# Value products ahead of the turning: one move in the order of TensorE's work in a sparse-attention loop

## The chip, the cores and the metric

The kernel runs on one core of one Trainium2 chip. The metric is the device time of one launch in microseconds (us). Before the change three runs gave 3794.74, 3799.57 and 3803.0 us, with a median of 3799.57. One execution was profiled; it took 3797.03 us, and its span, from the first recorded instruction to the last, is 3795.2 us. All numbers of the trace are from that execution.

## The reference

Two transformer blocks run on 512 tokens of width 1024. The first has a state-space branch and dilated attention; the second has two layers, each a feed-forward part, a token mixer and another feed-forward part. The token mixer computes a gated delta rule and a sparse attention from one projection of the input. The change lies in one part of the sparse attention: for a block of 128 queries, softmax attention over the keys of that block and those before it, in two forms (selected keys and a window), added to a third, compressed form:

```python
ss = jnp.einsum("bqgrd,bqgld->bgrql", qb, k_sel) * scale
p_sel = masked_softmax(ss, (tok <= t[:, None])[:, :, None])
o_sel = jnp.einsum("bgrql,bqgld->bqgrd", p_sel.astype(v_sel.dtype), v_sel)
sw = jnp.einsum("bqgrd,bkgd->bgrqk", qb, k_win) * scale
p_win = masked_softmax(sw, win_mask)
o_win = jnp.einsum("bgrqk,bkgd->bqgrd", p_win.astype(v_win.dtype), v_win)
o = gb[..., 0:1] * o_cmp + gb[..., 1:2] * o_sel + gb[..., 2:3] * o_win
```

With 512 tokens and 16 selected blocks of 64, every causal key is selected, and the window of 512 reaches all of them too; so both forms read the keys 0 to 128(qb+1) under one causal mask.

## The kernel before

Each engine has a program of its own, written out by hand in the order in which it runs; semaphores connect them, and an engine waits at the first instruction whose semaphore is not there. The function `pe_mix` is TensorE's program of the token mixer, `act_mix` ScalarE's and `dve_mix` VectorE's. They run once in each of the two layers.

The sparse attention is cut into 32 steps (`nsa_blocks`, `work`): four query blocks `qb`, four pairs of heads `j`, two forms `i`. Query block `qb` has n = qb + 1 key blocks of 128, so steps 0 to 7 have one key block, 8 to 15 two, 16 to 23 three and 24 to 31 four. Two heads run side by side (G = 0, 1). The work of step v goes through four engines' stages:

- `scores(v)`, L1868, TensorE: q times k into the PSUM banks `g[2]` and `g[3]`. It waits for `row_max` of step v-1, which tells that the banks have been read.
- `maxima(v)`, L2533, VectorE: masks the scores into `n_p` and takes the negative row maxima into `n_stat` (a custom instruction and a read of its accumulator, once for each G).
- `probs(v)`, L2253, ScalarE: exponentials in place in `n_p`, with their sums.
- `turned(v)`, L1879, TensorE: transposes the probabilities into `p[0]` and `p[1]`. It waits for the exponentials and for the copies of step v-1 (`n_tr0`, `n_tr1`).
- the copies of the transposes into `n_pt`: of G = 0 on ScalarE (L2261), of G = 1 on VectorE (L2568).
- `weighted(v)`, L1889, TensorE: probabilities times values into `p[2]` or `p[3]`. It waits for VectorE's adding of step v-2.
- `added(v)`, L2574 to L2585, VectorE: three small operations on the sums, then two that add the result to `n_y`.

The stages of neighbouring steps overlap. In loop step s TensorE issues `scores(s)`, `turned(s-1)`, `feed(("core", s))` and `weighted(s-2)`. VectorE issues `maxima(s)`, the copy of s-1, `convolved(("core", s))` and `added(s-2)`; after each query block it also squares and sums `n_y`. ScalarE issues the copy of s-1, `probs(s)` and `taps(("core", s))`.

`feed` puts pieces of another work between these: the projection of twelve channels of the delta rule, L364 to L366, three products of 512 columns for each of eight input blocks of a channel. A loop step takes one input block of it, from step 16 on two (`mix_points`). A channel is completed in steps 7, 15, 19, 23, 27 and 31. Then ScalarE scales it (`taps`, L2189) and, after every second channel, in steps 15, 23 and 31, splits the next weights (L358), whose low part POOL then makes (L350); VectorE convolves it with three long operations (`convolved`, L2441), which wait for ScalarE's scaling.

Of the kernel before, what the change touches and what calls it, by code (L numbers as in the profile page):

```python
# [1781 lines left out]
def nsa_blocks():  # L1782

    return [(qb, j, i) for qb in range(NB) for j in range(4) for i in range(2)]
# [34 lines left out]
def pe_mix(K, pe, pos):  # L1819
# [3 lines left out]
    work = nsa_blocks()  # L1823
# [6 lines left out]
    def feed(name):  # L1830
        for j in points.get(name, ()):
            h, k = j // KD, j % KD
            s, n = h // 2 % 2, h % 2
            if k == 0:
                if n == 0:
                    pe.wait_ge(K.sem("w_lo"), pos.next("w_lo"))
                pe.wait_ge(K.sem(f"g_free{n}"), pos.next(f"g_free{n}"))
            w = slice(k * 256 + n * P, k * 256 + n * P + P)
            last = three_pass(K, K.g[n][:], K.w_hi[:, s, w], K.w_lo[:, s, w], K.h_hi[:, k], K.h_lo[:, k], k == 0, k == KD - 1)
            if k == KD - 1:  # L1840
                last.then_inc(K.sem("part"), 1)
# [19 lines left out]
    def scores(v):  # L1861
        qb, j, i = work[v]
        w = (qb + 1) * P
        if v:
            pe.wait_ge(K.sem("row_max"), pos.next("row_max", 2))
        for G in range(2):
            r = slice(64 * G, 64 * G + 64)
            t.matmul(K.g[2 + G][:, 0:w], K.n_q[r, j, qb * P:qb * P + P], K.n_k[r, 2 + i, 0:w],  # L1868
                     start=True, stop=True).then_inc(K.sem("scores"), 1)

    def turned(v):
        n = work[v][0] + 1
        for G in range(2):
            pe.wait_ge(K.sem("n_pe"), pos.next("n_pe"))
            if v:
                pe.wait_ge(K.sem(f"n_tr{G}"), pos.next(f"n_tr{G}"))
            for k in range(n):
                o = G * n * P + k * P
                last = t.transpose(K.p[G][:, k * P:k * P + P], K.n_p[:, v % 2, o:o + P], ident)  # L1879
            last.then_inc(K.sem(f"n_pt{G}"), 1)  # L1880

    def weighted(v):
        qb, j, i = work[v]
        if v >= 2:
            pe.wait_ge(K.sem("n_acc"), pos.next("n_acc"))
        for G in range(2):
            pe.wait_ge(K.sem(f"n_tr{G}"), pos.value(f"n_tr{G}") + (1 if v == len(work) - 1 else 0))
            for k in range(qb + 1):
                last = t.matmul(K.p[2 + v % 2][:, 64 * G:64 * G + 64], K.n_pt[:, v % 2, 4 * G + k],  # L1889
                                K.m_v[:, k, P * i + 64 * G:P * i + 64 * G + 64], start=k == 0, stop=k == qb)  # L1890
        last.then_inc(K.sem("n_o"), 1)
# [125 lines left out]
    for step in range(len(work) + 2):  # L2017
        if 1 <= step < len(work):
            scores(step)
        if 1 <= step <= len(work):  # L2020
            turned(step - 1)
        feed(("core", step))
        if step >= 2:
            weighted(step - 2)
    pos.skip("row_max", 2)
    pos.skip("n_tr0")
    pos.skip("n_tr1")
# [699 lines left out]
def ffn_parts(conv, i, ada, norm, following):  # L2727
# [13 lines left out]
    ffn_c=ffn_parts(False, 2, lambda layer: None, lambda layer: Norm(layer, 2),  # L2741
                    lambda layer: Norm(layer + 1, 0) if layer + 1 < LAYERS else FINAL),
    mix=(pe_mix, act_mix, dve_mix), final=(pe_final, act_final, dve_final))
PE_PARTS, ACT_PARTS, DVE_PARTS = ({k: v[i] for k, v in PARTS.items()} for i in range(3))

# [184 lines left out]
```

## Time and profile before

| | |
|---|---|
| median of three runs | 3799.57 us |
| profiled execution | 3797.03 us, span 3795.2 us |
| TensorE busy | 3651.1 us, 96% of the span |
| VectorE, ScalarE, POOL busy | 1820.7, 1408.6, 1402.6 us |
| sparse-attention loop, layer 1 | about 1894 to 2021 us |
| sparse-attention loop, layer 2 | about 3092 to 3220 us |

A line of the trace names the engine (PE TensorE, PEld its weight loads, DVE VectorE, ACT ScalarE), the line of the kernel, the operation, the tile written and those read, and the shapes. A start is in us from the span's start; in brackets stands how long the engine had been idle, and what ended it. A busy time of neighbouring matmuls overlaps by some hundredths, so lengths are best read from start to start.

### The profile page before, as it was taken

The numbers are of one execution on the slowest core, as the hardware profiler recorded it, in microseconds if no ns is written. First come the engines' busy times: TensorE is split into PE (matmuls) and PEld (weight loads), VectorE is DVE, ScalarE is ACT, GpSimd is POOL, SyncE is SP. The second block draws the span as 40 slices with busy tenths as digits, with TensorE's granted clock in tenths as the row PEclk, the third lists the DMA queues.
The fourth block names the chain that finished last, engine by engine and source line by source line (L and its number), as shares of the span: only waits on it lengthen the run. The fifth ranks groups of instructions, "written<-read, shape, count | busy, mean of one in ns | idle before, by whom it ended". The sixth has DMA issues, their size and how long they took to land.

```text
span 3795.2 us, 48784 instructions
## 1 busy us (share of the span) xinstructions
PE 3651.1 (96%) x18948; PEld 3027.2 (80%) x18948; DVE 1820.7 (48%) x3285; ACT 1408.6 (37%) x2037; POOL 1402.6 (37%) x1092
## 2 busy tenths in 40 slices
PE   6999999999999999999998999999999989899998
PEld 5887878777788888887777978888888877888887
DVE  6887426665788664455375441123112457443111
ACT  5665424444322232223245432223222334533222
POOL 2333443223444444444211044455445411114444
PEclk9999999999999999999999999999999989999999
DMA  3211222111455655566100022223222401002222
GB/s 118 78 67 67 92 92 75 56 67 56 144 181 186 212 198 182 182 213 186 48 34 34 12 95 94 90 99 112 100 84 105 133 34 34 23 34 100 92 91 106
DMA packets 67647, 380.25 MB, mean 100 GB/s; under 512 B 7920, under 2 KB 8432, under 8 KB 39408
## 3 DMA queue, kind: packets, MB, share of 16 engines
q1 hardware_dynamic: 44192, 286.14, 21.2%
q10 hardware_dynamic: 23248, 91.19, 7.3%
q8 instruction: 149, 2.44, 0.3%
q14 instruction: 58, 0.48, 0.0%
HBM read 375.20 MB, written 2.10 MB: 99 GB/s over the span
## 4 chain that ended last, share of the span: by engine, by line
issue 62%; POOL 29%; PE 9%; POOLq 0%; DVE 0%; ACT 0%; DVEq 0%
POOL w_lo L350 29%; PE g L364 3%; PE g L365 3%; PE g L366 3%; POOLq L344 0%; DVE x L1696 0%; POOLq L347 0%; PE p L518 0%; PE p L510 0%; DVE x L1454 0%; DVE n_sq L497 0%; DVEq L155 0%; ACT n_sq L482 0%; POOLq L350 0%; ACT n_rc L525 0%
## 5 line engine op out<-in xcount | busy, mean ns | idle before, releaser
L350 POOL TENSOR_TENSOR w_lo<-w_raw,w_hi 128x512 fp32r<-128x512 f32 (+1 forms) x1088 | 1402.4, 1320 | 2386.3 <-ACT w_hi L358 2386.3
L364 PE MATMUL g<-h_hi,w_lo 128*128 128x512 f32 x2816 | 1135.6, 403 | 23.4 <-POOL w_lo L350 21.1
L365 PE MATMUL g<-h_lo,w_hi 128*128 128x512 f32 x2816 | 1106.7, 393 | 0.0
L366 PE MATMUL g<-h_hi,w_hi 128*128 128x512 f32 x2816 | 1106.3, 393 | 0.0
L358 ACT ACTIVATE w_hi<-w_raw 128x2048 fp32r<-128x2048 f32 (+1 forms) x292 | 515.8, 1766 | 968.6 <-PE g L366 931.8
L364 PEld LDWEIGHTS g<-h_hi,w_lo 128*128 128x128 f32 x2816 | 535.9, 190 | 144.3 <-POOL w_lo L350 24.4
L366 PEld LDWEIGHTS g<-h_hi,w_hi 128*128 128x128 f32 x2816 | 534.8, 190 | 115.6
L365 PEld LDWEIGHTS g<-h_lo,w_hi 128*128 128x128 f32 x2816 | 536.0, 190 | 109.9 <-issue 4.1
L364 PE MATMUL g<-act_hi,w_lo 128*128 128x512 f32 x880 | 346.0, 393 | 0.0
L366 PE MATMUL g<-act_hi,w_hi 128*128 128x512 f32 x880 | 342.9, 390 | 0.0
L365 PE MATMUL g<-act_lo,w_hi 128*128 128x512 f32 x880 | 342.5, 389 | 0.0
L1642 DVE TENSOR_TENSOR p<-f_acc,g 128x512 f32<-128x512 f32 x84 | 58.4, 696 | 566.5 <-PE g L366 565.3
L1490 DVE SCALAR_TENSOR_TENSOR p<-ada_w,csilu,p 128x256 f32<-128x256 f32 x432 | 211.7, 490 | 54.8 <-DMA ada_w<-in_ada 31.8
L366 PEld LDWEIGHTS g<-act_hi,w_hi 128*128 128x128 f32 x880 | 165.2, 188 | 35.4
L365 PEld LDWEIGHTS g<-act_lo,w_hi 128*128 128x128 f32 x880 | 165.4, 188 | 33.4
L364 PEld LDWEIGHTS g<-act_hi,w_lo 128*128 128x128 f32 x880 | 165.3, 188 | 33.3
L1454 DVE SCALAR_TENSOR_TENSOR x<-g,mods,x 128x512 f32<-128x512 f32 x48 | 36.0, 749 | 276.7 <-PE g L366 276.3
L1572 ACT ACTIVATE f_acc<-g 128x512 f32<-128x512 f32 x84 | 50.2, 598 | 258.8 <-PE g L366 250.2
L1621 DVE TENSOR_TENSOR act_lo<-p,act_hi 128x512 fp32r<-128x512 f32 x110 | 76.1, 692 | 119.2 <-ACT act_hi L1553 108.1
L497 DVE TENSOR_TENSOR n_sq<-n_sq 128x512 f32<-128x512 f32 x63 | 66.7, 1058 | 70.6 <-ACT n_sq L482 70.5
L482 ACT ACTIVATE n_sq<-x 128x512 f32<-128x512 f32 x72 | 44.9, 624 | 144.9 <-DVEq L1617 69.2
L1889 PEld LDWEIGHTS p<-m_v,n_pt 128*128 128x128 f32 x640 | 82.4, 194 | 8.5 <-DVE n_y L2585 3.3
(463 smaller groups left out, 4805.8 us busy)
## 6 DMA issues: line engine op xcount, KB each, us to landing
w_raw<-in_stream SPq DMA_DIRECT2D x212, 1024.0 KB, 4.8
ada_w<-in_ada ACTq DMA_DIRECT2D x144, 512.0 KB, 4.0
w_raw<-in_stream SPq DMA_DIRECT2D x80, 704.0 KB, 4.0
n_w<-in_w ACTq DMA_DIRECT2D x8, 1024.0 KB, 15.0
ada_w<-in_stream ACTq DMA_DIRECT2D x8, 512.0 KB, 4.4
x<-in_x SPq DMA_DIRECT2D x4, 512.0 KB, 9.7
b_w<-in_stream ACTq DMA_DIRECT2D x2, 1024.0 KB, 4.8
out_x<-x SPq DMA_DIRECT2D x4, 512.0 KB, 2.6
```

Of the source, the lines that this page charges most:

```text
L350: last = K.nc.gpsimd.tensor_tensor(K.w_lo[:, s, c], K.w_raw[:, s, c], K.w_hi[:, s, c].bitcast(F32), ALU.subtract)
L358: act.activation(K.w_hi[:, s, 0:width], K.w_raw[:, s, 0:width], ACT.Copy).then_inc(K.sem("w_hi"), 1)
L364: nc.tensor.matmul(out, w_lo, h_hi, start=start, stop=False)
L365: nc.tensor.matmul(out, w_hi, h_lo, start=False, stop=False)
L366: return nc.tensor.matmul(out, w_hi, h_hi, start=False, stop=stop)
L482: act.activation(K.n_sq[:, min(m, 1)], K.x[:, m], ACT.Square).then_inc(K.sem("sq"), 1)
L497: v.tensor_tensor(K.n_sq[:, 0], K.n_sq[:, 0], K.n_sq[:, 1], ALU.add).then_inc(K.sem("sq_added"), 1)
L1490: v.scalar_tensor_tensor(out, w[:, i * 256:i * 256 + 256], scalar(i), acc, ALU.mult, ALU.add).then_inc(pos.own, pos.tick())
L1572: act.activation(K.f_acc[:, s], K.g[2 * s][:], ACT.Silu).then_inc(K.sem("f_s"), 1)
L1621: v.tensor_tensor(K.act_lo[:, u], K.p[1 if conv else u % 2][:], K.act_hi[:, u].bitcast(F32), ALU.subtract).then_inc(K.sem("act_lo"), 1)
L1642: v.tensor_tensor(K.p[s][:], K.f_acc[:, s], K.g[2 * s + 1][:], ALU.mult).then_inc(K.sem("f_u"), 1)
L1889: last = t.matmul(K.p[2 + v % 2][:, 64 * G:64 * G + 64], K.n_pt[:, v % 2, 4 * G + k], K.m_v[:, k, P * i + 64 * G:P * i + 64 * G + 64], sta ...
```

## The change

In TensorE's loop `weighted(step - 2)` moves from the end of a step to the place between `scores(step)` and `turned(step - 1)`. Its wait for the copies is now for one more of each, since the turning that used to wait for the same copies just ahead of it comes later in the order.

```diff
@@ def weighted(v), in pe_mix
         for G in range(2):
-            pe.wait_ge(K.sem(f"n_tr{G}"), pos.value(f"n_tr{G}") + (1 if v == len(work) - 1 else 0))
+            pe.wait_ge(K.sem(f"n_tr{G}"), pos.value(f"n_tr{G}") + 1)
@@ the loop, in pe_mix
         if 1 <= step < len(work):
             scores(step)
+        if step >= 2:
+            weighted(step - 2)
         if 1 <= step <= len(work):
             turned(step - 1)
         feed(("core", step))
-        if step >= 2:
-            weighted(step - 2)
```

The other engines' rows are the same before and after. On TensorE, steps 15 and 16 of the first layer, from the end of step 14, read before (L1868 scores, L1879 turning, L364 to L366 projection, L1889 value products; two rows of equal operation and shape stand as one with a count):

```order
L1889 MATMUL p<-m_v,n_pt 128x64 x4
L1868 MATMUL g<-n_k,n_q 128x256 x2
L1879 MATMUL p<-masks,n_p 128x128 x4
L364 MATMUL g<-h_hi,w_lo 128x512
L365 MATMUL g<-h_lo,w_hi 128x512
L366 MATMUL g<-h_hi,w_hi 128x512
L1889 MATMUL p<-m_v,n_pt 128x64 x4
L1868 MATMUL g<-n_k,n_q 128x384 x2
L1879 MATMUL p<-masks,n_p 128x128 x4
```

and after, from the scores of step 15 on, with the same names:

```order
L1868 MATMUL g<-n_k,n_q 128x256 x2
L1889 MATMUL p<-m_v,n_pt 128x64 x4
L1879 MATMUL p<-masks,n_p 128x128 x4
L364 MATMUL g<-h_hi,w_lo 128x512
L365 MATMUL g<-h_lo,w_hi 128x512
L366 MATMUL g<-h_hi,w_hi 128x512
L1868 MATMUL g<-n_k,n_q 128x384 x2
L1889 MATMUL p<-m_v,n_pt 128x64 x4
L1879 MATMUL p<-masks,n_p 128x128 x4
```

The value products of step 13 stood behind the projection block that completes a channel in step 15, and now stand ahead of it. On TensorE the end of the loop, from the scores of step 31 on, reads before:

```order
L1868 MATMUL g<-n_k,n_q 128x512 x2
L1879 MATMUL p<-masks,n_p 128x128 x8
L364 MATMUL g<-h_hi,w_lo 128x512
L365 MATMUL g<-h_lo,w_hi 128x512
L366 MATMUL g<-h_hi,w_hi 128x512
L364 MATMUL g<-h_hi,w_lo 128x512
L365 MATMUL g<-h_lo,w_hi 128x512
L366 MATMUL g<-h_hi,w_hi 128x512
L1889 MATMUL p<-m_v,n_pt 128x64 x8
L1879 MATMUL p<-masks,n_p 128x128 x8
L1889 MATMUL p<-m_v,n_pt 128x64 x16
```

and after, with the same names:

```order
L1868 MATMUL g<-n_k,n_q 128x512 x2
L1889 MATMUL p<-m_v,n_pt 128x64 x8
L1879 MATMUL p<-masks,n_p 128x128 x8
L364 MATMUL g<-h_hi,w_lo 128x512
L365 MATMUL g<-h_lo,w_hi 128x512
L366 MATMUL g<-h_hi,w_hi 128x512
L364 MATMUL g<-h_hi,w_lo 128x512
L365 MATMUL g<-h_lo,w_hi 128x512
L366 MATMUL g<-h_hi,w_hi 128x512
L1889 MATMUL p<-m_v,n_pt 128x64 x8
L1879 MATMUL p<-masks,n_p 128x128 x8
L1889 MATMUL p<-m_v,n_pt 128x64 x8
```

The value products of step 29 move ahead of the last projection blocks, those of step 30 ahead of the last turning; those of step 31 stay last.

## Rows read from the trace of the kernel before

**Rows 1.** The page, part 1: busy us, share of the span, instructions.
```profile
PE 3651.1 (96%) x18948; PEld 3027.2 (80%) x18948; DVE 1820.7 (48%) x3285; ACT 1408.6 (37%) x2037; POOL 1402.6 (37%) x1092
```
**Rows 2.** TensorE's waits, whole span: us in total, times, longest.
```profile
PE g L1868 <- DVE n_stat L2533: 18.0, 10, 2.8
...
PE p L1889 <- DVE n_y L2585: 3.0, 2, 1.5
```
**Rows 3.** Timeline of TensorE, step 29 and the start of step 30.
```profile
1998.63 1.13 PE L1868 MATMUL g<-n_k,n_q 64*128 64x512 f32 x4
1999.69 1.09 PE L1879 MATMUL p<-masks,n_p 128*128 128x128 f32 x8
...
2002.01 1.89 PE L1889 MATMUL p<-m_v,n_pt 128*128 128x64 f32 x16
2003.83 1.13 PE L1868 MATMUL g<-n_k,n_q 64*128 64x512 f32 x4
```
**Rows 4.** Timelines of TensorE, ScalarE and VectorE, steps 15 to 17.
```profile
1935.46 1.00 PE L1889 MATMUL p<-m_v,n_pt 128*128 128x64 f32 x8
...
1936.01 0.77 ACT L2189 ACTIVATE m_qk<-g,cols,cols 128x512 f32<-128x512 f32 x1
...
1936.39 0.92 PE L1868 MATMUL g<-n_k,n_q 64*128 64x384 f32 x4
...
1936.81 2.32 DVE L2441 SCALAR_TENSOR_TENSOR m_qk<-g,cols,m_qk 128x511 f32<-128x511 f32 x3 [1.32 <-ACT m_qk L2189]
...
1942.54 0.42 DVE L2568 COPY n_pt<-p 128x256 f32<-128x256 f32 x1
...
1942.68 0.92 PE L1868 MATMUL g<-n_k,n_q 64*128 64x384 f32 x4 [2.56 <-DVE n_stat L2533]
```
**Rows 5.** Timeline of TensorE, from the end of step 7 to step 9.
```profile
1909.52 0.55 PE L1889 MATMUL p<-m_v,n_pt 128*128 128x64 f32 x4
1910.00 0.70 PE L1868 MATMUL g<-n_k,n_q 64*128 64x256 f32 x4
...
1914.93 1.23 PE L1868 MATMUL g<-n_k,n_q 64*128 64x256 f32 x4 [2.78 <-DVE n_stat L2533]
```
**Rows 6.** Timelines of TensorE and VectorE, steps 19 to 21.
```profile
1953.82 1.45 PE L1889 MATMUL p<-m_v,n_pt 128*128 128x64 f32 x12
...
1959.24 0.55 DVE L2568 COPY n_pt<-p 128x384 f32<-128x384 f32 x1
...
1959.51 0.92 PE L1868 MATMUL g<-n_k,n_q 64*128 64x384 f32 x4
```
**Rows 7.** The same engines: scores of step 25, copy in step 28, last products.
```profile
1978.27 1.13 PE L1868 MATMUL g<-n_k,n_q 64*128 64x512 f32 x4 [1.20 <-DVE n_stat L2533]
...
1997.36 0.69 DVE L2568 COPY n_pt<-p 128x512 f32<-128x512 f32 x1
...
2018.41 2.48 PE L1889 MATMUL p<-m_v,n_pt 128*128 128x64 f32 x16 [1.49 <-DVE n_y L2585]
```
**Rows 8.** Timeline of TensorE, scores of steps 11 and 13.
```profile
1922.63 0.70 PE L1868 MATMUL g<-n_k,n_q 64*128 64x256 f32 x4
...
1928.13 0.70 PE L1868 MATMUL g<-n_k,n_q 64*128 64x256 f32 x4
```
**Rows 9.** Four stretches: length, busy by engine, granted clock, DMA share, GB/s.
```profile
1914.00:1920.00 6.00, 5.07 (x19) 3.68 (x19) 4.21 (x23) 2.45 (x9) 0.00 (x0) 0.50 0.01 3
1921.00:2019.00 98.00, 92.75 (x613) 74.09 (x612) 72.37 (x242) 50.84 (x124) 13.60 (x11) 1.00 0.07 22
2020.00:2023.00 3.00, 3.00 (x11) 2.52 (x11) 2.79 (x10) 1.83 (x4) 0.28 (x1) 0.50 0.47 131
3177.00:3180.00 3.00, 3.00 (x13) 1.92 (x10) 2.25 (x9) 1.10 (x4) 0.11 (x1) 0.50 0.57 147
```
**Rows 10.** Waits of the first layer's loop, and the page's part 5: weight loads.
```profile
PEld p L1879 <- issue: 11.2, 20, 0.8
...
L1889 PEld LDWEIGHTS p<-m_v,n_pt 128*128 128x128 f32 x640 | 82.4, 194 | 8.5 <-DVE n_y L2585 3.3
```

## The prediction

> **What bounds the kernel now.** I read four views in this order. The page's first part says TensorE is busy 96% of the span [rows 1]: what it waits for is what there is to win or lose, and a wait added to it lengthens the program. TensorE's list of waits then shows what it waits for in the sparse-attention steps, which are the only place of these lines: 18.0 us in ten waits at the score products, all for VectorE's row maxima, and 3.0 us in two at the value products [rows 2]. That is 9.0 and 1.5 us a layer.
>
> The timeline of a late step shows what a step looks like without a wait [rows 3]. Scores at 1998.63, turnings at 1999.69, value products at 2002.01, next scores at 2003.83: 1.06 us of scores, 2.32 of turnings and two projection blocks, 1.82 of value products, each beginning where the one before stops. So in an undisturbed step the order of the four pieces is worth nothing: their sum stays.
>
> The timeline where TensorE does wait shows the cause [rows 4]. In step 15 a projection channel is completed. ScalarE scales it (1936.01), VectorE convolves it (1936.81, 2.32 us), and only then does VectorE add a step's result and take the maxima of step 16; they end at 1942.54, where the copy behind them begins, and TensorE's scores of step 17 start at 1942.68 after 2.56 us of waiting. A channel is completed six times a layer, in steps 7, 15, 19, 23, 27 and 31. I call the chain from the completed projection over ScalarE's scaling and VectorE's convolution to the next maxima the convolution chain.
>
> **The change part by part.** The instructions are the same on every engine; only TensorE's order changes, and the transfers, the splitting of weights and the other engines' orders stay. In a step s the value products of s-2 now stand ahead of the turning of s-1, and so ahead of the projection blocks.
>
> *The convolution chain starts later.* The projection that completes a channel now has one more set of value products before it in its step. ScalarE's scaling waits for that projection and, in its own order, for the copy and the exponentials of the step, which follow the turnings. Both parents come later by the length of one set of value products, whichever is the later. Everything behind the scaling is unchanged in length, so the chain's end moves by that length too. The products that used to stand between this projection and the delayed scores are now ahead of it, so TensorE has as much less to do in the meantime. I read the length from the start of the products to the start of the next scores: 0.48 us with one key block (1909.52 to 1910.00) [rows 5], 0.93 with two (1935.46 to 1936.39) [rows 4], 1.37 with three (the row has 1.45 [rows 6]; the rows of one, two and four blocks, 0.55, 1.00 and 1.89, exceed the distance to the next scores by 0.07), 1.82 with four [rows 3].
>
> Step by step, per layer:
> - Step 7: the value products of step 5, one block, +0.48; the wait of 2.78 [rows 5] becomes 3.26.
> - Step 15: two blocks, +0.93; 2.56 becomes 3.49 [rows 4].
> - Step 19: three blocks, 1.37. TensorE does not wait here now. The maxima end at 1959.24, the scores could start 0.14 later as in the case above, at 1959.38, and start at 1959.51 [rows 6]. The slack is 0.13, so +1.24.
> - Step 23: three blocks, +1.37; 1.20 becomes 2.57 [rows 7].
> - Step 27: four blocks, 1.82. The maxima end at 1997.36 [rows 7], the scores start at 1998.63 [rows 3]: slack 1.13, so +0.69.
> - Step 31: four blocks, +1.82. The last value products wait 1.49 for VectorE's adding behind the last convolution [rows 7], and this becomes 3.31.
>
> Together 0.48 + 0.93 + 1.24 + 1.37 + 0.69 + 1.82 = 6.53 us a layer, 13.1 in two. The rest of a layer's 9.0 us at the scores (9.0 - 2.78 - 2.56 - 1.20 = 2.46) lies at the loop's start, where VectorE still works on what came before the loop; I leave it as it is, with 0.5 a layer either way as its bound.
>
> *The clock.* After the wait of 2.78 TensorE's granted clock is 0.50, the lower level of 1.2 GHz, and it is 1.00 from 1921 to 2019, a stretch with the waits of 2.56 and 1.20 in it; it is 0.50 again behind the 1.49 at the end, and in the second layer also behind the 1.20 (3177 to 3180) [rows 9]. So short waits go either way, and the longest takes the clock down. A low stretch costs: from the scores at 1914.93 to those at 1922.63 two steps take 7.70 us, the next two, of the same shape, 5.50 (to 1928.13) [rows 5, 8], a difference of 2.2. The wait behind step 15 grows to 3.49, past the 2.78 that dropped the clock: I add 2.2 in each layer, 4.4. Those behind steps 19, 23 and 27 end at or under 2.57, about the 2.56 that dropped nothing: I take 0 for them. Behind step 31 the clock is low already in one of the layers shown: 0 too. Bounds: -2 (a wait behind which it is low now keeps it high, by another phase) to +17.6 (the rule below).
>
> [...]
>
> *The hand-overs between pieces.* Scores now follow projections instead of value products, value products follow scores, turnings follow value products. The trace shows none of the last two. A hand-over can cost or spare at most about one exposed weight load, 0.19 us [rows 10], over 62 steps some -11.9 to +11.9. Now and then one hand-over goes into short, load-bound products out of long streaming, and one goes the other way, so I take 0, and a fifth of the bound for the range.
>
> *The wait that moves.* The value products now themselves wait for ScalarE's and VectorE's copies of the turned probabilities of s-2; before, the turning just ahead had waited for them. Behind that wait stand turning and projections. VectorE makes its copy right behind the maxima that release the scores (0.42 at 1942.54 against scores of 0.92 [rows 4]; 0.69 at 1997.36 against 1.13 [rows 3, 7]), so it is done when the scores are: 0, and if that cover failed, some 0.1 in the six disturbed steps. VectorE's adding gets its products earlier and needs them no earlier, as it stands behind the convolution: 0.
>
> The sum: 13.1 + 4.4 + 0 = 17.5. The profiled execution took 3797.0 us around a span of 3795.2, and lies 2.5 below the median of the runs, 3799.57. So 3814.5 from its own time, 3817.1 from the median; I say 3816.
>
> **The rivals.**
> - *Faster: the value products fill a wait between scores and turnings.* In the first layer TensorE's weight loads stand idle 11.2 us before the turnings, in 20 steps [rows 10]. If the matmuls stood too, the value products would fill this: 22.4 us in two layers, less the 13.1, 3788. It decides if in an undisturbed step the turnings start later than the scores stop streaming. Against it: the scores of 1.13 at 1998.63 still stream when the turnings start at 1999.69, and the same 1.06 recurs with no wait named [rows 3]. The idle loads lie under streaming scores.
> - *Slower still: every lengthened wait drops the clock.* New low stretches behind steps 15, 19, 27 in both layers, behind 23 in the first and behind 31 in the second, 8 times 2.2 = 17.6 in place of 4.4: 3829. For it: the 1.20 and the 1.49 did it once each [rows 7, 9]. Against it: the 2.56 never.
> - *No change: the chain is not moved.* If ScalarE's scaling hung on something that the order doesn't shift, or the slow clock let VectorE catch up behind each wait, only the undisturbed half of the growth would be left, some 6.5: 3804. For it: VectorE waits less for value products. Against it: both parents of the scaling stand behind the moved products in TensorE's order.
>
> **How the numbers follow.** Two runs of this kernel can differ by about 0.2%, 7.6 us, so under 3807 counts as no change. Forecast 0.66, the slow clock everywhere 0.14, no change 0.14, filled waits 0.06. The forecast's own range: 13.1 less 1.0 for the start, 2 for the clock and 2.4 for the hand-overs at the low end, 3804.7; at the high end 17.5 + 2.4 + half of the clock's further 13.2 + 2.6 for the median, 3826. With the second rival and the spread of runs it reaches from 3804 to 3830. Faster 0.06, same 0.14, slower 0.80.
>
> **What would show it.** In the changed profile the waits of the scores for VectorE should sum to about 13.7 us a layer in place of 9.0, with new ones near 1.2 behind step 19 and near 0.7 behind step 27; the wait of the last value products should be near 3.3; between the scores' start and the scaling of a completed channel there should be one set of products more; an undisturbed late step should still take 5.20. It is wrong if the undisturbed step gets longer or shorter (a hand-over), if the waits behind steps 15 and 23 don't grow, or if turnings are found to have waited before.

## The result, and the profile after

The changed kernel takes 3828.3 us (median of five runs, 3816.73 to 3830.19) against 3800.04 (3794.74 to 3803.37): a ratio of 1.0067 over all runs, with a 95% interval of 1.0055 to 1.0078 (the two medians alone give 1.0074). It is slower by 21 to 30 us, and its time lies inside the predicted 3804 to 3830, near the upper end and 12 us above the 3816 that was forecast.

The profiled execution's span is 3822.6 us, 27.3 more than before. Cut at the scores of step 1 and the end of the last value products of each loop, it goes like this (differences are taken before rounding):

| us | before | after | difference |
|---|---|---|---|
| up to the first loop | 1894.3 | 1901.3 | +7.0 |
| first loop | 126.6 | 141.3 | +14.7 |
| between the loops | 1071.4 | 1068.0 | -3.4 |
| second loop | 127.9 | 138.9 | +11.1 |
| behind it | 575.0 | 573.1 | -2.0 |

Only the loops hold changed code, and they account for 25.7 us. What lies outside them differs by 1.6 in sum, from one execution to another.

TensorE's list of waits (us in total, times, longest), to set against [rows 2]:

```profile
PE g L1868 <- DVE n_stat L2533: 26.1, 14, 3.4
...
PE p L1889 <- DVE n_y L2585: 6.4, 2, 3.2
```

32.5 us where there were 21.0, and four waits more. The timeline of steps 15 to 17 shows one that grew, to set against [rows 4]:

```profile
1944.15 0.92 PE L1868 MATMUL g<-n_k,n_q 64*128 64x384 f32 x4
...
1944.61 0.76 ACT L2189 ACTIVATE m_qk<-g,cols,cols 128x512 f32<-128x512 f32 x1
...
1945.41 2.32 DVE L2441 SCALAR_TENSOR_TENSOR m_qk<-g,cols,m_qk 128x511 f32<-128x511 f32 x3 [1.42 <-ACT m_qk L2189]
...
1951.15 0.42 DVE L2568 COPY n_pt<-p 128x256 f32<-128x256 f32 x1
...
1951.29 0.98 PE L1868 MATMUL g<-n_k,n_q 64*128 64x384 f32 x4 [3.37 <-DVE n_stat L2533]
```

From the scaling to the delayed scores it takes 6.68 us, before 6.67: the chain is as long as it was. But the scores of step 16 now start 0.46 us ahead of the scaling, where they started 0.38 behind it, so TensorE is through with its work 0.84 us sooner relative to the chain, and waits 3.37 in place of 2.56. The other grown waits, behind steps 7, 23 and 31, and the two new ones, behind steps 19 and 27:

```profile
1922.37 1.22 PE L1868 MATMUL g<-n_k,n_q 64*128 64x256 f32 x4 [3.10 <-DVE n_stat L2533]
...
1972.59 0.92 PE L1868 MATMUL g<-n_k,n_q 64*128 64x384 f32 x4 [1.01 <-DVE n_stat L2533]
...
1992.82 1.97 PE L1868 MATMUL g<-n_k,n_q 64*128 64x512 f32 x4 [2.43 <-DVE n_stat L2533]
...
2017.20 1.13 PE L1868 MATMUL g<-n_k,n_q 64*128 64x512 f32 x4 [0.47 <-DVE n_stat L2533]
...
2038.88 1.54 PE L1889 MATMUL p<-m_v,n_pt 128*128 128x64 f32 x6 [3.22 <-DVE n_y L2585]
```

An undisturbed late step, to set against [rows 3]:

```profile
2006.15 1.13 PE L1868 MATMUL g<-n_k,n_q 64*128 64x512 f32 x4
2007.21 2.00 PE L1889 MATMUL p<-m_v,n_pt 128*128 128x64 f32 x16
2009.04 1.04 PE L1879 MATMUL p<-masks,n_p 128*128 128x128 f32 x8
2009.84 0.48 PE L364 MATMUL g<-h_hi,w_lo 128*128 128x512 f32 x1
...
2011.40 1.13 PE L1868 MATMUL g<-n_k,n_q 64*128 64x512 f32 x4
```

It takes 5.25 us in place of 5.20. From scores to value products it is 1.06, as it was from scores to turnings; value products 1.83 (1.82), turnings 0.80 (0.85 in the timeline before, whose first projection starts at 2000.54), but the two projections 1.56 where they were 1.47. Scores behind projections start later than value products did.

Stretches of the first loop, and two of the second, behind steps 15 and 23 (columns as in [rows 9], the granted clock is third from the end):

```profile
1922.00:1928.00 6.00, 5.63 (x20) 3.58 (x20) 4.47 (x20) 2.45 (x9) 0.00 (x0) 0.50 0.01 4
1929.00:1951.00 22.00, 18.93 (x125) 13.71 (x123) 15.72 (x64) 11.11 (x34) 3.74 (x4) 1.00 0.00 1
1952.00:1958.00 6.00, 6.00 (x24) 4.76 (x22) 4.33 (x17) 1.78 (x7) 0.21 (x1) 0.50 0.48 175
1959.00:1992.00 33.00, 30.38 (x194) 22.79 (x192) 21.10 (x67) 14.05 (x34) 3.51 (x3) 1.00 0.00 1
1993.00:1999.00 6.00, 6.00 (x25) 4.50 (x24) 2.61 (x10) 1.28 (x5) 0.47 (x1) 0.50 0.50 178
2000.00:2037.00 37.00, 35.19 (x233) 26.93 (x231) 23.42 (x69) 16.95 (x37) 1.20 (x1) 1.00 0.00 1
2038.00:2046.00 8.00, 7.12 (x25) 6.35 (x26) 5.40 (x16) 4.23 (x8) 2.75 (x3) 0.50 0.36 131
3161.00:3166.00 5.00, 5.00 (x19) 4.03 (x18) 3.49 (x14) 1.68 (x5) 0.00 (x0) 0.50 0.59 210
3202.00:3207.00 5.00, 5.00 (x21) 3.68 (x18) 2.11 (x8) 0.20 (x2) 0.00 (x0) 0.50 0.58 213
```

The clock is at its lower level, 0.50, behind the waits of 3.10, 3.37, 2.43 and 3.22, and at 1.00 through those of 1.01 and 0.47. Before, two such stretches lay in this loop, the second of them mostly behind its end. What two of the new stretches cost can be read from these scores, those of steps 19 and 26, behind the scores of steps 17 and 25 shown above:

```profile
1962.75 0.92 PE L1868 MATMUL g<-n_k,n_q 64*128 64x384 f32 x4
...
2000.88 1.13 PE L1868 MATMUL g<-n_k,n_q 64*128 64x512 f32 x4
```

Steps 17 and 18 take 11.46 us, and step 25 takes 8.06.

### The profile page after: what moved, and what is told of

It is laid out like the page before. It is cut to its first block, busy times and chain, and to the rows that moved or that the text cites. A ratio compares the mean times of both kernels' runs of the same rounds, so it can differ in the third digit from the quotient of the medians.

```text
span 3822.6 us, 48784 instructions
## 1 busy us (share of the span) xinstructions
PE 3665.7 (96%) x18948; PEld 3025.9 (79%) x18948; DVE 1822.5 (48%) x3285; ACT 1407.3 (37%) x2037; POOL 1402.6 (37%) x1092
## 4 chain that ended last, share of the span: by engine, by line
issue 62%; POOL 28%; PE 9%; POOLq 0%; DVE 0%; ACT 0%; DVEq 0%
POOL w_lo L350 28%; PE g L364 3%; PE g L365 3%; PE g L366 3%; POOLq L344 0%; DVE x L1696 0%; POOLq L347 0%; PE p L518 0%; PE p L510 0%; DVE x L1454 0%; DVE n_sq L497 0%; DVEq L155 0%; ACT n_sq L482 0%; POOLq L350 0%; ACT n_rc L525 0%
## 5 line engine op out<-in xcount | busy, mean ns | idle before, releaser
L364 PE MATMUL g<-h_hi,w_lo 128*128 128x512 f32 x2816 | 1137.6, 404 | 24.6 <-POOL w_lo L350 22.4
L366 PE MATMUL g<-h_hi,w_hi 128*128 128x512 f32 x2816 | 1108.8, 394 | 0.0
L364 PEld LDWEIGHTS g<-h_hi,w_lo 128*128 128x128 f32 x2816 | 537.0, 191 | 145.8 <-POOL w_lo L350 25.6
L366 PEld LDWEIGHTS g<-h_hi,w_hi 128*128 128x128 f32 x2816 | 535.7, 190 | 116.1
L364 PE MATMUL g<-act_hi,w_lo 128*128 128x512 f32 x880 | 346.1, 393 | 0.0
L366 PE MATMUL g<-act_hi,w_hi 128*128 128x512 f32 x880 | 342.9, 390 | 0.0
L366 PEld LDWEIGHTS g<-act_hi,w_hi 128*128 128x128 f32 x880 | 165.1, 188 | 35.5
L364 PEld LDWEIGHTS g<-act_hi,w_lo 128*128 128x128 f32 x880 | 165.3, 188 | 33.4
L1889 PEld LDWEIGHTS p<-m_v,n_pt 128*128 128x128 f32 x640 | 82.9, 205 | 37.7 <-DVE n_y L2585 18.4
```

What stands on the lines that cost most here:

```text
L364: nc.tensor.matmul(out, w_lo, h_hi, start=start, stop=False)
L366: return nc.tensor.matmul(out, w_hi, h_hi, start=False, stop=stop)
```

## The experiments

Each run is compared with runs of the kernel before on the same chip (medians 3798.4, 3801.3 and 3799.6 us in three groups). "Loops" is the sum of both loops in the profiled execution, cut as in the table: 254.5 us before, 280.2 with the change.

**Old order in the six steps alone.** The change is undone where a channel is completed; `early` decides for each step where its value products stand. (`weighted` is also told which place it has, for its wait for the copies; that part is left out here.)

```diff
+        early = step not in (7, 15, 19, 23, 27, 31)
+        if step >= 2 and early:
+            weighted(step - 2, True)
         if 1 <= step <= len(work):
             turned(step - 1)
         feed(("core", step))
+        if step >= 2 and not early:
+            weighted(step - 2, False)
```

> The new order in all steps but the six that complete a projection channel (7, 15, 19, 23, 27, 31), which keep the old one. Theory (the change costs by the convolution chain that starts a set of value products later, and by the slow clock behind the longer waits): TensorE's waits at scores and last value products go back from some 16 us a layer to the 10.5 of before, the clock's low stretches to those of before, and only the hand-overs between pieces remain, 0.05 to 0.06 us in some 50 steps, 3 us in all: about 3803 us (3798 to 3808). Rival (the new order costs in every step, whatever the convolution does): 26 of 32 steps keep it, so about 26/32 of the 28 us stay: 3823.

3803.4 us, ratio 1.001 (0.9999 to 1.0021); loops 258.2. The waits:

```profile
PE g L1868 <- DVE n_stat L2536: 17.0, 9, 2.7
...
PE p L1889 <- DVE n_y L2588: 2.9, 2, 1.4
```

19.9 us, a little under the 21.0 of before. Twenty-six of 32 steps have the new order, and nearly all of the loss is gone: the interval reaches just below 1.

**New order in the six steps alone.** One line differs from the run before:

```diff
-        early = step not in (7, 15, 19, 23, 27, 31)
+        early = step in (7, 15, 19, 23, 27, 31)
```

> The old order in all steps but the six that complete a projection channel, which get the new one. Theory: the waits of the full change, some 16 us a layer, and its low clock behind steps 7, 15 and 23; the hand-overs of the other steps are as before. The full change less its 3 us of hand-overs: about 3823 us (3814 to 3829). Rival (the new order costs in every step): 6/32 of 28 us, 3805.

3817.3 us, ratio 1.0048 (1.0035 to 1.0061); loops 271.1. The waits:

```profile
PE g L1868 <- DVE n_stat L2536: 25.8, 13, 3.4
...
PE p L1889 <- DVE n_y L2588: 6.3, 2, 3.2
```

32.1 us, those of the full change, from six steps in 32. With the run before, the place of the loss is shown. It lies 6 us under the expectation's middle: the expectation had the clock low behind step 23, and here it stays up behind the same wait (2.45 us), in this stretch of the first layer and in that of the second:

```profile
1987.00:2028.00 41.00, 38.09 (x256) 30.51 (x254) 26.77 (x80) 19.82 (x43) 2.29 (x2) 1.00 0.07 27
3193.00:3233.00 40.00, 37.18 (x251) 29.86 (x248) 25.82 (x76) 19.64 (x41) 2.21 (x2) 1.00 0.08 27
```

**Value products behind the turnings, ahead of the projections.** Made on the kernel before.

```diff
         if 1 <= step <= len(work):
             turned(step - 1)
-        feed(("core", step))
         if step >= 2:
             weighted(step - 2)
+        feed(("core", step))
```

> In every step scores, turnings, value products, projections: the value products still ahead of the projections, but behind the turnings, so that copies and exponentials are where they were before. Theory (the completed projection is the parent of the scaling that counts, the exponentials only as far as they end later): waits of some 15.5 us a layer, near the full change; in steps 7 and 15 a little under it, since there the exponentials end 0.1 to 0.4 us after the projection now. About 3820 us (3812 to 3828). Rival (what costs is that the turnings and with them the exponentials come later): waits stay at 10.5 us a layer, 3800.

3823.6 us, ratio 1.0058 (1.0044 to 1.0073); loops 277.9. The waits, and the scores of step 17:

```profile
PE g L1868 <- DVE n_stat L2533: 24.7, 14, 3.0
...
PE p L1889 <- DVE n_y L2585: 6.3, 2, 3.2
```
```profile
1947.55 1.65 PE L1868 MATMUL g<-n_k,n_q 64*128 64x384 f32 x4 [3.02 <-DVE n_stat L2533]
```

31.0 us in all, though turnings, copies and exponentials stand where they stood before. So the projection that comes later is enough; only where the exponentials ended later than it, as in step 15, is the wait shorter (3.02 against 3.37).

**Scaling and convolution in the next step, old order.** Made on the kernel before.

```diff
@@ ScalarE's loop
+        taps(("core", step - 1))
         if 1 <= step <= len(work):
             turned(step - 1)
         if 1 <= step < len(work):
             probs(step)
-        taps(("core", step))
@@ VectorE's loop
-        convolved(("core", step))
+        convolved(("core", step - 1))
```

> The kernel before, but ScalarE scales a completed channel at the start of the next step, ahead of that step's copy and exponentials, and VectorE convolves it in the next step, behind its copy: the convolution finds its input ready. Theory (the waits come from VectorE standing idle for the scaled channel, 1.3 to 1.5 us each time, and then convolving late): the waits behind steps 15, 19, 23, 27 and of the last value products vanish or fall under 1 us, behind step 7 some 1.5 to 2 us stay, as do the 2.5 at the loop's start; 10.5 us a layer become 4 to 5, and the low clock behind the loop's waits mostly goes: 12 us of waits and 4 to 6 of clock less, about 3783 us (3775 to 3791). Rival (VectorE has too much work in these steps, whenever the channel comes): waits as before, 3800.

3782.5 us, ratio 0.995 (0.9937 to 0.9964); loops 234.6. Its only waits at these places, the convolution of the channel that step 15 completes, and the granted clock of both loops:

```profile
PE g L1868 <- DVE n_stat L2533: 9.1, 8, 1.8
```
```profile
1937.54 2.31 DVE L2441 SCALAR_TENSOR_TENSOR m_qk<-g,cols,m_qk 128x511 f32<-128x511 f32 x3
```
```profile
1897.00:2013.00 116.00, 111.47 (x736) 88.78 (x737) 89.79 (x333) 62.18 (x169) 17.59 (x15) 1.00 0.08 28
3085.00:3202.00 117.00, 112.42 (x746) 89.64 (x745) 90.53 (x334) 63.16 (x171) 18.24 (x15) 1.00 0.08 28
```

VectorE has the same work in a step as before, but no longer stands idle for the scaled channel: this convolution starts without a wait, where it waited 1.32 us [rows 4]. So it is that idle time, and not the amount of VectorE's work, that most of the waits come from: TensorE waits 9.1 us in place of 21.0, and the clock stays up.

**The same in the new order.** The edit of the run before, on the changed kernel.

> The changed kernel, with the scaling and the convolution of a completed channel moved to the next step as in the run before (ScalarE scales ahead of its copy and exponentials, VectorE convolves behind its copy). Theory (the new order costs through the late convolution; besides that only its hand-overs, 0.055 us in each of 62 steps, 3.4 us): beside that same move in the old order (3782) it costs the hand-overs and some 3 us a layer of waits, as the turnings and copies still come later in a step: about 3792 us (3787 to 3799), under the kernel before. Rival (the new order costs the 28 us in every step, whatever the convolution does): 3810.

3790.6 us, ratio 0.9964 (0.995 to 0.9977); loops 241.8. The new order is no longer slower than the kernel before. Against the run before its loops are 7.2 us longer. It has 2.3 us more waits, 10.0 at the scores and 1.4 at value products, which now wait for ScalarE's copy; its late steps take 5.25 us against 5.20; and one low stretch of the clock, 3.4 us long, lies in its first layer. So with the convolution a step later, the new order still costs some 7 us of the 25.7.

**Two more moves on VectorE.** Added to the old order with scaling and convolution in the next step: the convolution that stood ahead of the loop goes into step 1, and the squares of a finished query block go five steps later.

```diff
-    convolved("turn")
...
-        convolved(("core", step - 1))
+        convolved("turn" if step == 1 else ("core", step - 1))
...
-            if step % 8 == 1:
-                squares((step - 2) // 8)
+            if step in (14, 22, 30, 33):
+                squares((step - 10) // 8 if step < 33 else 3)
```

> The old order with scaling and convolution in the next step (3782 us), and two further moves on VectorE alone: the convolution that stands ahead of the loop goes behind the copy of loop step 1, and the squares of a finished query block go from the second step of the next block to its seventh. Theory (every wait of the scores in the loop is VectorE's convolving or squaring ahead of the maxima): the wait of 0.6 at the scores of step 11 goes, the 1.8 at the start moves by a step and shrinks by about 1 us: 2 to 4 us less, about 3779. Rival (the waits at the loop's start are of another cause): 3782.

3778.5 us, ratio 0.9938 (0.992 to 0.9956); loops 232.7, with 5.5 us of waits. It is the fastest kernel here, under the one before and the changed one. Beside the 0.995 of the run without these two moves, on another chip, the intervals overlap; that it is faster than that one stays open.

**Extra products in the changed kernel's waits.** They keep TensorE busy while it waits; nothing reads them. They overwrite `p[0]`, so they wait for ScalarE's copy of it first.

```diff
+    def warm(step):
+        n = {9: 11, 17: 13, 21: 3, 25: 9, 33: 12}.get(step, 0)
+        if n:
+            pe.wait_ge(K.sem("n_tr0"), pos.value("n_tr0") + 1)
+        for _ in range(n):
+            t.matmul(K.p[0][:], K.mask_r[:, 2], K.h_hi[:, 0], start=True, stop=True)
     for step in range(len(work) + 2):
+        warm(step)
```

> The changed kernel with extra products of 128 by 512 that nothing reads, put into TensorE's longest waits: 11 ahead of the scores of step 9, 13 of step 17, 3 of step 21, 9 of step 25, 12 ahead of the last value products. They fill most of each wait and end inside it, so nothing that waits comes later by them. Theory (what the waits and hand-overs of 15 us leave of the change's cost is the slow clock behind the waits): the granted clock stays 1.00 in the loop, and the loop loses what it pays for the low stretches: loops of 280.2 us less 32.5 of waits less 3.4 of hand-overs stand against 225.5 of a loop with no low stretch, so 18.8 us go, about 3809 us (3802 to 3816). Rival (that rest is of another cause, such as contention): 3828 or more.

3811.9 us, ratio 1.0026 (1.0016 to 1.0037). The time is as the clock theory has it, 16 us under the change. The profiled execution was the slowest of the twelve, 3827.7 with loops of 283.8, and does not show what was expected:

```profile
1901.00:1927.00 26.00, 26.00 (x96) 18.84 (x95) 14.43 (x70) 8.23 (x37) 3.19 (x3) 0.50 0.11 41
1928.00:2038.00 110.00, 107.62 (x681) 81.17 (x679) 77.15 (x255) 52.52 (x130) 14.38 (x12) 1.00 0.05 20
```

Behind the filled waits the clock is 1.00, but it fell at the loop's start, behind a wait of 1.82 us that had been left unfilled, and stayed low there.

**Extra products in the old kernel's waits.** The same on the kernel before, with 10, 10, 4 and 5 products in steps 9, 17, 25 and 33.

> The kernel before with such extra products in its waits: 10 ahead of the scores of step 9, 10 of step 17, 4 of step 25, 5 ahead of the last value products. Theory (clock): its loops of 254.5 us less 21.0 of waits stand against the same 225.5, so 8.0 us of low clock go: about 3791 us (3786 to 3796). Rival (another cause): 3799 or more.

3794.5 us, ratio 0.9976 (0.9965 to 0.9987); loops 247.8, at a clock of 1.00. Useless work in its waits makes the kernel before 6.7 us faster, in the loops and in the medians. The scores of steps 9 and 11:

```profile
1919.59 0.70 PE L1868 MATMUL g<-n_k,n_q 64*128 64x256 f32 x4 [0.41 <-DVE n_stat L2541]
...
1924.91 0.70 PE L1868 MATMUL g<-n_k,n_q 64*128 64x256 f32 x4 [0.19 <-DVE n_stat L2541]
```

With the clock up, steps 9 and 10 take 5.32 us, where they took 7.70.

**Waits filled from the loop's start.** Added: 5 products in step 2 and 2 in step 4 of the changed kernel.

> The changed kernel with its waits filled as in the run before, and also the two at the loop's start: 5 extra products ahead of the scores of step 2, 2 ahead of those of step 4. In the profiled execution of the run before, the clock fell behind the wait of 1.8 us at step 2 and stayed low for 27 us, in both layers. Theory (it was that wait that let it fall, and the filled ones behind it don't): no low stretch is left in the loops, each takes about 261.4 / 2 = 130.7 us (129 to 133), and the whole about 3808 us (3800 to 3813). Rival (the extra products themselves bring the low stretch, or the rest of the change's cost is no clock): a low stretch again, or loops of 138 us and more without one.

3810.0 us, ratio 1.0024 (1.0012 to 1.0035); loops 131.0 and 131.3. Both loops, a stretch with heavy transfers, and the scores of steps 17, 19, 25 and 26:

```profile
1895.00:2025.00 130.00, 126.24 (x795) 94.78 (x794) 95.12 (x337) 63.87 (x173) 20.07 (x16) 1.00 0.07 25
3099.00:3229.00 130.00, 125.99 (x792) 94.49 (x792) 94.85 (x336) 63.64 (x172) 19.73 (x16) 1.00 0.07 25
1942.00:1950.00 8.00, 8.00 (x52) 5.94 (x50) 7.28 (x27) 3.80 (x12) 0.73 (x1) 1.00 0.39 132
```
```profile
1941.78 0.92 PE L1868 MATMUL g<-n_k,n_q 64*128 64x384 f32 x4 [0.46 <-DVE n_stat L2541]
...
1950.07 0.92 PE L1868 MATMUL g<-n_k,n_q 64*128 64x384 f32 x4
...
1980.16 1.13 PE L1868 MATMUL g<-n_k,n_q 64*128 64x512 f32 x4 [0.39 <-DVE n_stat L2541]
...
1984.97 1.13 PE L1868 MATMUL g<-n_k,n_q 64*128 64x512 f32 x4
```

No low stretch is left. The changed loops shrink from 280.2 to 262.3 us by added work alone, so the low clock cost them 17.9. Steps 17 and 18 take 8.29 us in place of 11.46, and step 25 takes 4.81 in place of 8.06. Transfers are not what made these steps slow: they run in steps 17 and 18 here too, at 132 GB/s from 1942 to 1950, and the steps are no longer for it.

## Why the prediction was right, and where its terms were off

The mechanism is the one forecast: the completed projection comes one set of value products later, the convolution chain with it, and TensorE waits at the next scores. The two runs that split the six steps from the others show the place, the two runs with the scaling in the next step show the cause. The direction and the place came as forecast, the size did not: the sum was 17.5 us, and the loops lost 25.7, in three terms.

- *The waits: forecast 13.1, measured 11.5* (32.5 less 21.0). Step by step, first layer, forecast and measured: 3.26 and 3.10, 3.49 and 3.37, 1.24 and 1.01, 2.57 and 2.43, 0.69 and 0.47, 3.31 and 3.22. All six forecasts are 0.09 to 0.23 high there. A new step is itself 0.05 longer, and the delayed scores are due two steps on, which would cover 0.1 of it.
- *The hand-overs: forecast 0, measured about 3.1* (0.05 us in 62 steps). The step "one goes into short products out of long streaming, and one goes the other way, so I take 0" failed: it weighed the pieces that follow long streaming, and not that scores begin later behind projections than value products do (1.56 against 1.47), which the turnings behind value products give back only in part (0.80 against 0.85). The late step of 5.25 us in place of 5.20 is what the prediction itself had named as a sign of being wrong. Why scores start later there is not shown.
- *The clock: forecast 4.4, measured 11.2* (17.9 of the change less 6.7 of before). This term was mis-sized most, in the number of low stretches and in their price. The step that took 0 for the wait behind step 23, "about the 2.56 that dropped nothing", failed: 2.43 dropped it in both layers, as 3.22 did at the end. A length of wait that had left the clock up once was no bound for another place. The price of 2.2 was a misreading: steps 9 and 10 are not "of the same shape" as 11 and 12, since step 9 has the value products of step 7, with one key block. Against the filled kernel they lost 2.4 (7.70 less 5.32), and later stretches cost more: 3.2 in steps 17 and 18 (11.46 less 8.29), and 3.2 in step 25 (8.06 less 4.81). Compared in this way step by step, both layers, with the clock's loss of the kernel before taken off, the stretches behind step 15 make 6.3, those behind step 23 4.8 and the loop's end 1.1, while a shorter one behind step 7 in the second layer gives back 1.0.

11.5 + 3.1 + 11.2 = 25.8, against 25.7. The clock's term is what the filled kernels leave, so this sum checks only the other two: without the clock, 262.3 less 247.8 is 14.5, against 14.6.

Of the rivals, the filled waits between scores and turnings failed: no matmul of a turning is in TensorE's list of waits, before or after. The idle time of their weight loads, 11.2 us a layer before [rows 10], is gone from that place in the changed kernel, and no time was won by it. "No change" failed with the grown waits. The slow clock behind every lengthened wait holds, in both layers, behind four waits of six and fails behind the short ones, 1.01 and 0.47 in the first layer. The Trainium skill ("TensorE: Matmul & The Clock Gate", "HAM oscillation — how this bites in real kernels") tells of a kernel in which the wait for a transfer ahead of each group of matmuls sent the engine back to the slow clock. Here waits of 2.43 to 3.37 us, for VectorE, did so in the changed kernel, though 2.45 did not in the run with the new order in six steps alone.

That rival's 3829 is within 1 us of the median, and this is luck: its sum of 30.7 us (13.1 and 17.6) stands against 25.7 in the loops. The forecast itself, 3816, was 12 us low. The time lies inside the range because the range had been stretched to 3830 to take in that rival; the forecast's own range ended at 3826.

## What to carry to other kernels

Where an engine is never idle in the steady loop, an order within a step is worth little there (0.05 us in 5.2 here); look for the few steps in which another engine does extra work, and ask how a move shifts the start of that work. Here a late consumer was better served by taking its input a step later and finding it ready than by either order of its producer: that made this kernel 0.5% faster where the reordering made it 0.7% slower. And a wait of two or three microseconds costs more than its length where it takes the clock down: in these loops 11.5 us of added waits brought 11.2 us of slow clock.

## What was not expected of the hardware

Products that nobody reads, put into waits, shortened the program by 6.7 us before the change and by some 16 to 18 after it. In one profiled execution the clock fell behind a wait of 1.8 us and stayed at 0.50 for 26 us, though TensorE was busy for all 26.00 of them; with that wait filled it stayed at 1.00. Other executions show the same wait with the clock up, and the two runs that split the six steps from the others show it low for 3.4 us behind it, in their second layer. So what lets the clock stay low so long is open.
